# Seven block products in place of eight in the up projections of two squared-ReLU feed-forwards

## The reference, cut to what matters

```python
D_FF_2 = 4 * D_MODEL          # 4096; D_MODEL = 1024, SEQ = 512

def sq_relu_mlp(h, w1, w2):
    u = jax.nn.relu(h @ w1)
    return (u * u) @ w2
...
        x = x + sq_relu_mlp(rms_norm(x, norm_mlp[i]), mlp_w1[i], mlp_w2[i])
```

## Time and profile before

| what | value |
|---|---|
| median of 3 executions | 2276.53 us (2275.1 to 2276.61) |
| span of the profiled execution | 2272.1 us |
| left around the span, to the median | 4.4 us |
| TensorE busy | 2247.1 us, 99% of the span |
| VectorE, ScalarE, GpSimd busy | 54%, 34%, 7% |
| share of TensorE in the chain that ended last | 93% |

### The profile page before, as it was taken

The page is one execution under the profiler, slowest core; times in us unless marked ns, Lnnn a source line. Parts: engine busy times, 40 slices in busy tenths (PEclk is TensorE's granted clock), DMA queues, the critical chain, the costliest instruction groups (busy, mean ns, idle before and its releaser), DMA issues.

```text
span 2272.1 us, 28489 instructions
## 1 busy us (share of the span) xinstructions
PE 2247.1 (99%) x11659; PEld 1825.8 (80%) x11659; DVE 1230.8 (54%) x1464; ACT 777.3 (34%) x1024; POOL 168.5 (7%) x135
## 2 busy tenths in 40 slices
PE   9999999999999999999999999999999999999999
PEld 7888888878888888887876788888877868888888
DVE  6434446597543355575567644344468864544443
ACT  4222234244422323353247322222334573212221
POOL 2000001030100100020011100000101201000000
PEclk9999999999999999999999999999999999999999
DMA  5223223310323232232320232232233102323322
GB/s 188 93 93 106 97 79 99 93 61 20 102 92 105 82 109 93 75 110 93 104 65 20 78 107 93 93 100 87 87 106 89 61 20 65 102 93 95 108 86 81
DMA packets 193332, 200.56 MB, mean 88 GB/s; under 512 B 6370, under 2 KB 187378, under 8 KB 193236
## 3 DMA queue, kind: packets, MB, share of 16 engines
q1 hardware_dynamic: 193236, 199.22, 27.7%
HBM read 191.93 MB, written 2.10 MB: 85 GB/s over the span
## 4 chain that ended last, share of the span: by engine, by line
PE 93%; DVE 5%; ACT 1%; issue 1%; DMA 0%; SPq 0%; DVEq 0%; ACTq 0%
PE psum L684 92%; DVE sm L2477 1%; DVE rstd L1976 0%; DVE w_lo L296 0%; PE psum L1165 0%; PE psum L1173 0%; DVE free_x L1958 0%; ACT free_h L1449 0%; DVE free_h L1961 0%; DVE free_x L2599 0%; DVE sm L2597 0%; DVE sm L2303 0%; PE psum L916 0%; DVE xg_lo L1958 0%; DMA gains<-in_gains 0%
## 5 line engine op out<-in xcount | busy, mean ns | idle before, releaser
L684 PE MATMUL psum<-xg_lo,w_hi 128*128 128x512 f32 (+1 forms) x1576 | 608.4, 389 | 0.4 <-ACT free_x L1449 0.4
L684 PE MATMUL psum<-xg_hi,w_hi 128*128 128x512 f32 (+1 forms) x1528 | 596.0, 390 | 4.3 <-DVE xg_lo L1958 1.7
L684 PE MATMUL psum<-xg_hi,w_lo 128*128 128x512 f32 (+1 forms) x1528 | 592.9, 388 | 0.0
L288 ACT ACTIVATE w_hi<-w_raw 128x2048 fp32r<-128x2048 f32 (+1 forms) x178 | 338.7, 1903 | 478.0 <-PE psum L684 478.0
L296 DVE TENSOR_TENSOR w_lo<-w_raw,w_hi 128x2048 fp32r<-128x2048 f32 (+1 forms) x176 | 403.5, 2293 | 162.2 <-ACT w_hi L288 159.0
L684 PE MATMUL psum<-h_hi,w_hi 128*128 128x512 f32 x1144 | 451.7, 395 | 0.3 <-DVE h_lo L1958 0.3
L684 PE MATMUL psum<-h_hi,w_lo 128*128 128x512 f32 x1144 | 445.6, 389 | 0.0
L684 PE MATMUL psum<-h_lo,w_hi 128*128 128x512 f32 x1144 | 445.6, 389 | 0.0
L684 PEld LDWEIGHTS psum<-xg_lo,w_hi 128*128 128x128 f32 x1576 | 295.6, 188 | 62.2 <-ACT free_x L1449 1.4
L684 PEld LDWEIGHTS psum<-xg_hi,w_hi 128*128 128x128 f32 x1528 | 286.9, 188 | 68.9 <-issue 4.6
L684 PEld LDWEIGHTS psum<-xg_hi,w_lo 128*128 128x128 f32 x1528 | 286.9, 188 | 59.1
...
## 6 DMA issues: line engine op xcount, KB each, us to landing
w_raw<-in_mlp_w SPq DMA_DIRECT2D x64, 1024.0 KB, 5.4
w_raw<-in_ffn_w_gate SPq DMA_DIRECT2D x21, 1024.0 KB, 5.3
w_raw<-in_ffn_w_up SPq DMA_DIRECT2D x21, 1024.0 KB, 5.3
w_raw<-in_ffn_w_down SPq DMA_DIRECT2D x16, 1024.0 KB, 5.2
w_raw<-in_diff_w_in SPq DMA_DIRECT2D x12, 1024.0 KB, 5.1
w_raw<-in_w_in SPq DMA_DIRECT2D x9, 1024.0 KB, 5.2
w_raw<-in_dsa_w_in SPq DMA_DIRECT2D x9, 1024.0 KB, 5.1
...
```

The lines of the kernel that those rows point to most:

```text
L288: e.activation(w_hi[:, c % 2, 0:n], w_raw[:, c % 2, 0:n], ACT.Copy).then_inc(sem("hi_done"), 1)
L684: return pe.matmul(out, lhsT, rhs, start=start, stop=stop)
```

## The change

A pair of up blocks is one product of a 1024x512 weight piece with the 1024x512 normed input. It is cut in halves along the outputs (two blocks), the inputs (even and odd tiles) and the tokens (two times 256). Plainly that is eight block products; the changed kernel does seven, on sums of the halves, for all pairs but the first of each layer: 7 pairs in mlp0 and 7 in mlp1, in groups of 1, 2, 2 and 2.

- **TensorE** (`fast_up`): seven products of 24 matmuls of 128x256 each, in place of 96 of 128x512. They go to three banks; the loop is written out.
- **Weights**: each product has its own "strip" of 1024 columns (half a block) in one of four places of `w_hi` and `w_lo`. `strip_hi` and `strip_lo` split it. Strip n waits for product n-4 to be done with its place. Strips 5 and 6 count `hi_done`, `lo_done` and `pe_blk` as a block did.
- **Loads** (`fast_loads`): five transfers of half a block per pair in place of two of a whole one; one quarter (`w2` even rows) comes twice.
- **GpSimd** (`fast_sums`): four in-place sums of 128x1024 per pair: `w_first`, `w_next`, `w_third`, `w_next`.
- **Input sums**: `x_split` and `x_low` make four sums of the input's quarters for each of four tile pairs, once a layer, in the first pair's `square_pair`. ScalarE scales two tiles into `x_raw`, VectorE makes four differences of 128x256, ScalarE rounds them (`sx_hi`), VectorE subtracts (`sx_lo`).
- **Outputs**: ScalarE copies three partial results per pair (two into `buf_c` and `buf_d`, one from bank to bank); VectorE adds, rectifies with the norm's factor and leaves the square to ScalarE (in place in `buf_a`, `buf_b`). In the first pair of a layer the old form stays.
- **Order at the ends**: block numbers and sides of `w_hi` are tied by `wside`; the two down blocks behind a group wait for the strip that frees their side (`freed_by`). The down blocks wait for the hidden tiles in three steps, not two.
- Many one-off semaphores are joined (`const_a`, `const_b`, `const_c` to `const_in` and the like), with the same waits or later ones far from any use.

The core of the diff. In order: the new tiles; where a strip comes from and what it waits for; the loads; TensorE's seven products; the down blocks' waits; ScalarE's `x_split`, `fast_up` and `square_pair`; VectorE's `x_split`, `x_low`, `fast_up` and `square_pair`; GpSimd's sums (`add_rows(dst, src, done)` adds `src` to `dst`). `split(n)` is `strip_hi` on ScalarE and `strip_lo` on VectorE, for strips 4 and up. `last_quarter` takes the last 128x512 out of a bank and counts `evac`; `hidden_hi` and `hidden_lo` split the 128x1024 hidden tiles.

```diff
+        sx_hi = nc.alloc_sbuf_tensor_at("sx_hi", [P, 4, KT // 2, TS], F32R, offset=arena_at)
+        sx_lo = nc.alloc_sbuf_tensor_at("sx_lo", [P, 4, KT // 2, TS], F32R, offset=arena_at + 4096 * 4)
+        sx_raw = nc.alloc_sbuf_tensor_at("sx_raw", [P, 4, KT // 2, TS], F32, offset=arena_at + 4096 * 4)
+        w_run = [arena[:, 8192 + 1024 * i:9216 + 1024 * i] for i in range(2)]
+        w_third = sq[:].rearrange("p a t -> p (a t)")
...
+        def strip_source(c0, n):
+            pair, i = fast_groups[c0][n // 7], n % 7
+            c = pair_block[pair]
+            if i == 0:
+                return raw(c, 0), (sem(f"landed{c % 2}"), 16 * (c // 2 + 1))
+            if i == 3:
+                return raw(c + 1, 0), (sem(f"landed{(c + 1) % 2}"), 16 * ((c + 1) // 2 + 1))
+            if i == 5:
+                return raw(c + n // 7 % 2, 1), (sem("w22_in"), 16 * (pair + 1))
+            if i == 4:
+                return w_third, (sem("w_third"), STEP * (pair + 1))
+            return w_run[run_half[pair]], ((sem("w_first"), STEP * (pair + 1)) if i == 1 else
+                                     (sem("w_next"), STEP * (2 * pair + (1 if i == 2 else 2))))
...
+            src, ready = strip_source(c0, n)
+            e.wait_ge(*ready)
+            if n < 4:
+                e.wait_ge(sem("pe_blk"), c0 - 1 + n // 2)
+            else:
+                e.wait_ge(*strip_mark("pe", c0, n - 4))
+            e.activation(strip(c0, n)[0], src, ACT.Copy).then_inc(strip_mark("hi", c0, n)[0], 1)
...
+                e.wait_ge(*strip_mark("pe", *freed_by[c]))
...
+                for q, pair in enumerate(fast_groups[c0]):
+                    c = c0 + 2 * q
+                    w1, w2 = blocks(q)
+                    if q == 0:
+                        sp.wait_ge(sem("lo_done"), c0 - 1)
+                    else:
+                        sp.wait_ge(*strip_mark("lo", c0, 7 * (q - 1) + 1))
+                    half(raw(c, 0), w1, 0, sem(f"landed{c % 2}"))
+                    if q > 1:
+                        sp.wait_ge(*strip_mark("lo", c0, 7 * (q - 2) + 6))
+                    if run_half[pair]:
+                        sp.wait_ge(*x_sums_ready(p, 3))
+                    half(w_run[run_half[pair]], w2, 0, sem("w21_in"))
+                    if q < 2:
+                        sp.wait_ge(sem("lo_done"), c0 - 1 + q)
+                    if q:
+                        sp.wait_ge(*strip_mark("lo", c0, 7 * (q - 1) + 2))
+                    half(raw(c + q % 2, 1), w2, 1, sem("w22_in"))
+                    if q == 0:
+                        sp.wait_ge(sem("ssq_done"), 7 * (p + 1))
+                    else:
+                        sp.wait_ge(*strip_mark("lo", c0, 7 * (q - 1) + 4))
+                    half(w_third, w2, 0, sem("w21_third_in"))
+                    if q == 0:
+                        sp.wait_ge(sem("lo_done"), c0)
+                    else:
+                        sp.wait_ge(*strip_mark("lo", c0, 7 * (q - 1) + 6))
+                    half(raw(c + 1, 0), w1, 1, sem(f"landed{(c + 1) % 2}"))
...
+                    def product(i):
+                        dst = {1: side_sum, 3: first_sum, 5: side_sum}.get(i, run)
+                        fresh = i < 2
+                        wh, wl = strip(c0, 7 * q + i)
+                        pe.wait_ge(*strip_mark("lo", c0, 7 * q + i))
+                        for k in range(KT // 2):
+                            for m in range(2):
+                                cols = slice(k * BC + m * P, k * BC + (m + 1) * P)
+                                (w0, w1), (a0, a1) = (wh[:, cols], wl[:, cols]), moving(i, k)
+                                out_ = dst[:, m * TS:(m + 1) * TS]
+                                pe.matmul(out_, w0, a0, start=fresh and (k, m) == (0, 0), stop=False, skip_group_check=True)
+                                pe.matmul(out_, w0, a1, start=False, stop=False, skip_group_check=True)
+                                last = pe.matmul(out_, w1, a0, start=False, stop=(k, m) == (KT // 2 - 1, 1), skip_group_check=True)
+                        last.then_inc(strip_mark("pe", c0, 7 * q + i)[0], 1)
+                    pe.wait_ge(sem("evac"), c0 - 1 if q == 0 else c0 + 2 * q - 2)
+                    product(0)
+                    if q == 0:
+                        pe.wait_ge(*x_sums_ready(p, 3))
+                    product(1)
+                    pe.wait_ge(sem("p_copied"), 3 * pair + 1)
+                    product(2)
+                    product(3)
+                    pe.wait_ge(sem("p_copied"), 3 * pair + 3)
+                    product(4)
+                    product(5)
+                    pe.wait_ge(sem("u_read"), pair + 1)
+                    product(6)
...
+                        waits = {0: [(sem("h_done"), h0 + tiles // 2 - 2)], tiles - 4: [(sem("h_done"), h0 + tiles // 2 - 1)],
+                                 tiles - 2: [(sem("h_done"), h0 + tiles // 2)]}
...
+            def x_split(p, i):
+                n = 4 * fast_turn(p) + i
+                if i:
+                    act.wait_ge(sem("x_sums"), 5 * n - 1)
+                for m in range(2):
+                    a(x_raw[:, m, :], x_res[:, 2 * i + m, :], ACT.Copy,
+                      scale=ngain(p, 2 * i + m)).then_inc(sem("x_scaled"), 1)
+                act.wait_ge(sem("x_sums"), 5 * n + 4)
+                a(sx_hi[:, :, i, :], sx_raw[:, :, i, :], ACT.Copy).then_inc(sem("x_scaled"), 1)
...
+                for q in range(len(made)):
+                    split(7 * q + 3)
+                    square(q - 1, 0)
+                    copy(q, 0)
+                    split(7 * q + 4)
+                    hidden_hi(q - 1, 0)
+                    copy(q, 1)
+                    split(7 * q + 5)
+                    square(q - 1, 1)
+                    copy(q, 2)
+                    split(7 * q + 6)
+                    hidden_hi(q - 1, 1)
+                    for n in range(7, 10):
+                        split(7 * q + n)
+                q = len(made) - 1
+                hi(act, after)
+                for s_ in range(2):
+                    square(q, s_)
+                    hidden_hi(q, s_)
+                hi(act, after + 1)
...
+                    def square_pair():
+                        hi(act, c + 2)
+                        for i in range(2):
+                            x_split(p, i)
                         for s_ in range(2):
-                            act.wait_ge(sem("hmul"), 2 * j + (h0 + s_ + 1))
-                            a(hidden(p)[0][:, bass.ds(4 * j + 2 * s_, 2), :], buf_d[:], ACT.Copy).then_inc(sem("h_hi_done"), 1)
-                            if s_ or not first:
-                                hi(act, c + 2 + s_, j)
-
-                    pair, n_pairs = (gated_pair, tiles // 2) if gated else (square_pair, tiles // 4)
-                    if g == 0:
-                        pair(0, first=True)
+                            act.wait_ge(sem("hmul"), h0 + s_ + 1)
+                            a(hidden(p)[0][:, 2 * s_:2 * s_ + 2, :], buf_d[:], ACT.Copy).then_inc(sem("h_hi_done"), 1)
+                            if s_ == 0:
+                                for i in range(2, 4):
+                                    x_split(p, i)
+                            else:
+                                hi(act, c + 3)
...
+            def x_split(p, i):
+                n = 4 * fast_turn(p) + i
+                dve.wait_ge(sem("x_scaled"), 3 * n + 2)
+                even, odd, z = x_raw[:, 0, :], x_raw[:, 1, :], sx_raw[:, :, i, :]
+                e1, e2, o1, o2 = even[:, 0:TS], even[:, TS:S], odd[:, 0:TS], odd[:, TS:S]
+                tt(z[:, 0, :], o2, e2, ALU.subtract).then_inc(sem("x_sums"), 1)
+                tt(z[:, 3, :], e1, e2, ALU.subtract).then_inc(sem("x_sums"), 1)
+                dve.wait_ge(sem("x_sums"), 5 * n + 1)
+                stt(z[:, 1, :], z[:, 0, :], -1.0, e1, ALU.mult, ALU.subtract).then_inc(sem("x_sums"), 1)
+                dve.wait_ge(sem("x_sums"), 5 * n + 3)
+                stt(z[:, 2, :], o1, -1.0, z[:, 1, :], ALU.mult, ALU.subtract).then_inc(sem("x_sums"), 1)
+            def x_low(p, i):
+                dve.wait_ge(sem("x_scaled"), 3 * (4 * fast_turn(p) + i + 1))
+                tt(sx_lo[:, :, i, :], sx_raw[:, :, i, :], sx_hi[:, :, i, :].bitcast(F32),
+                   ALU.subtract).then_inc(sem("x_sums"), 1)
...
+                for q, pair in enumerate(made):
+                    run, side_sum, first_sum = pair_banks(c0, q)
+                    last_quarter(q - 1)
+                    split(7 * q + 3)
+                    split(7 * q + 4)
+                    hidden_lo(q - 1, 0)
+                    split(7 * q + 5)
+                    split(7 * q + 6)
+                    hidden_lo(q - 1, 1)
+                    dve.wait_ge(*strip_mark("pe", c0, 7 * q + 3))
+                    dve.wait_ge(sem("h_done"), h0 + 2 * q)
+                    rectify(buf_b, by_halves(first_sum), slice(0, TS), ALU.max).then_inc(sem("hmul"), 1)
```

(61 more changed lines are left out.)

292 lines of the change are left out of this document (220 added, 72 removed).

## The result

The change makes the kernel slower: 2315.23 us (median of 4, 2312.08 to 2319.95) against 2275.82 us beside it (2274.34 to 2276.61), a ratio of 1.0177 [1.0163, 1.0192]. That is 39.4 us more where 31 was forecast; 2308 was said, and 2315.23 lies in the range. The profiled execution took 2314.29 us, its span is 2312.3 us, 40.2 more than before.

A forecast was written before the change was run, and what follows sets the result against it. TensorE, busy 99% of the span, was taken as the bound. Full-group pairs -19.2, their ends +2.4, first groups +46.2 and clock +2 gave +31.4 on 2272.1, a span of 2303.5 and a median of 2308 us; range 2293 to 2325.

The forecast's parts named there:

- twelve pairs in full groups: Pairs in the six groups of two: TensorE saves 1.60 us a pair, -19.2 us in all.
- ends of the full groups: First down block behind each two-pair group starts late, by 0.4 us a group (bounds 0 to 2): +2.4 us.
- first groups: Each layer's one-pair first group waits for the input sums and costs 23.1 us, saving counted: +46.2 us.
- clock: TensorE's clock falls in the holes at layer starts: 1 us a layer, +2 us in all.
- What TensorE saves: Seven products at 0.120 us a matmul make a pair 20.16 us instead of 21.76: 1.60 us less.
- The start of a layer: First group of mlp0 and mlp1: TensorE idles 9.7, 8.7, 3.4 and 3.0 us behind the input sums' chain.
- The lockout: VectorE stands still while GpSimd adds; at a layer's start two GpSimd sums cut into the differences, 2 x 2.5 = 5.0 us.
- At nothing: Extra DMA of 3.5 MB a layer, half-block loads, written-out loops and joined semaphores were said to cost nothing.
- The input sums are hidden: Rival at layer starts: sums ready when the second product wants them, so -14 us, 2262 us; chance 0.04.
- Both engines become the bound in every pair: Rival in running pairs: VectorE and GpSimd alternate and bound them, 22 to 53 us more, 2330 and up; chance 0.12.
- The clock stays down: Rival: TensorE's clock stays low after the holes, 2 x 2.9 us a layer, 2318 us; chance 0.10.
- GpSimd does not cut in: Rival at layer starts: GpSimd's sums come earlier or later than the input sums, 10 us less, 2298 us; chance 0.08.

The follow-up runs named there:

- e4: Changed kernel with the first down block's load, in the six two-pair groups, released by strip 8's lo instead of strip 12's: 2302.61 us, ratio 1.0115.
- e12: Changed kernel with GpSimd's sums of weights made over 2 columns in place of 1024: 2290.70 us, ratio 1.0072.
- e7: Changed kernel with input sums made in group 0's down blocks, first groups left plain, and first down block's load released by strip 8's lo: 2255.17 us, ratio 0.9903.
- e1: Changed kernel without the input sums, their products reading the plain input: 2281.48 us, ratio 1.0021.
- e8: e7 with GpSimd's sums of weights over 2 columns in place of 1024: 2254.43 us, ratio 0.9903.

## Why the prediction was right, and where it was off

The mechanism was the forecast one; of its terms one was far too small. By its own terms, on the span:

| term | forecast | measured |
|---|---|---|
| twelve pairs in full groups | -19.2 | -21.7 (6 x 3.61, from e4) |
| ends of the full groups | +2.4 | +13.6 |
| first groups | +46.2 | +48.1 with the clock |
| clock | +2 | in the row above |
| sum | +31.4 | +40.0 |

**What TensorE saves.** Forecast 1.60 us a pair, measured 1.80. Three of the seven products have the token blocks' pitch of 0.120 us, four have 0.118: 24 x (4 x 0.118 + 3 x 0.120) = 20.0 us, and 21.76 - 20.0 = 1.8. The prediction named another pitch as a sign of being wrong and foresaw full groups nearly without holes. The first came out a little against it, by 0.002 us in four products of seven, the second more, with the holes of 1.2 to 2.7 us below.

**The start of a layer.** Forecast 23.1 and 1 for the clock, measured 22.5 and 1.5 to 1.6. The chain holds row by row, with the 0.33 us of offset added: the evacuation of block c forecast for 1317.3, seen at 1316.55; the last `sx_lo` ready at 1330.2 and 1329.25; the first down block's lo at 1353.8 and 1352.7. The lockout was taken as 5.0 us and was 4.4. The four holes were forecast as 9.7, 8.7, 3.4 and 3.0, and are 8.9, 5.9, 0.9 and 3.2. The prediction said that the slow products "run slow for nothing, since they are followed by longer waits". For the first that is so, and its 2 us and more come out of the second hole. The second ran slow into the third hole, which shrank to 0.9 for that reason. The clock's loss proper is the 1.6 us in the first down block. So the total agrees to 0.1 us partly because a chain 0.6 us too long and a clock loss 0.6 too small cancel.

**The ends of the groups** are the term that was mis-sized: "I take 0.4 us a group" was 1.4 to 4.4. The hand-run queue was right to the tenth where it went (the lo ready 40.7 us into the group; 1436.77 + 2.29 - 1398.38 = 40.68). What it lacked:

- TensorE is done earlier. Where nothing holds it (e4) the first down block starts 39.7 us into the group, not 40.3, for the pitch of 0.118 and because the group's products start 0.2 us before the evacuation from which it is counted.
- The first down block also waits for the addition out of the sixth product's bank, which stands behind that lo in VectorE's queue: 0.7 us more. This wait is in `begin`, and the prediction did not list it.
- The load landed 5.4 to 7.0 us after its release, and the two late ones (7.0 and 6.8) make some 2.6 us of the sum.
- Behind one hole the clock fell: 1.6 us.

The first two give 40.7 + 0.7 - 39.7 = 1.7 us a group, against 1.78 read for mlp0's group 1. e4 shows that the late load is the cause of all of it, and e12 that the load has no slack because of GpSimd's sums. Why two loads landed late stays open.

**At nothing.** The double quarter, the halves of loads and the written-out loops cost nothing that e7 shows. The first down block's load was not free, as above.

**The rivals.** *The input sums are hidden*: false; e1 prices them at 15.6 us a start. *Both engines become the bound in every pair*: false as a matter of throughput, since e7 and e8 agree and a strip stretches from 1.22 to 3.31 us and the groups' time doesn't change. But the same alternation costs some 20 us in the changed kernel by lateness: the 24.5 of e12 less 3 to 5 for its better clock, or, by group, 2 x 4.4 at the starts and 12.0 at the ends. The slack inside a pair was enough (the prediction found 1.2 us at the tightest), and there was none behind the last one. *The clock stays down*: in small part, 1.5 to 1.6 us a start and 1.6 at one group's end, not the 5.8 us a layer of the rival. What the Trainium skill ("TensorE: Matmul & The Clock Gate", What's actually happening) says of an idle array losing its clock, the windows above show too (0.83, then 0.50 in a hole of 8.9 us); the windows from 1330 and 1336 also show the return, from 0.50 to 1.00, which no row of the kernel before could. *GpSimd does not cut in*: false, 2.44 and 2.57 us at exactly the differences.
